# Differential heads between plain heads, `pv` taken out a step later, and the norm of the differential half inside the attention

## The reference, cut to what matters

```python
# plain heads (one block of 256 keys, so plain causal attention), q and k normed and rotated
p = softmax(mask(q @ k.T * 64 ** -0.5));  a = p @ v                       # 8 heads, v of width 64
a_out = rms_norm(a, moba_out_gain)                                        # over each head's 64
# differential heads: two maps of scores each
p0, p1 = softmax(mask(q0 @ k0.T / 8)), softmax(mask(q1 @ k1.T / 8))
b = (p0 - lam * p1) @ v                                                   # 4 heads, v of width 128
b_out = rms_norm(b, diff_out_gain) * (1.0 - lambda_init)                  # over each head's 128
x = x + concatenate([a_out, b_out]) @ w_out
x = x + peer_ffn(rms_norm(x, ffn_norm), ...)                              # experts
# second block, memory attention: keys and values of the memory, which need nothing of x
k, v = split(rmsnorm(mem, norm_mem_g) @ w_kv)
```

## Time and profile before

| | us |
|---|---|
| runs | 1474.99 median of 3, 1472.27 to 1475.25 |
| profiled execution, its own time | 1471.86 |
| its span in the trace | 1470.1 |
| busy in the span: PE, DVE, ACT, POOL | 1254.2, 801.9, 597.7, 904.9 |
| first scores, start of `xv0`, first `mixT` transpose, start of `w_out` | 99.37, 165.55, 182.82, 186.15 |
| TensorE idle before 162.43, released by DVE L1393 | 2.23 |
| ACT square of `att` (L984), 128 x 2048, at 166.47 | 1.92 |
| first gather, last product of the experts | 240.67, 930 |

### The profile page before, as it was taken

How to read it: one execution, slowest core, us unless ns; L and a number is a source line. 1 busy time by engine, 2 the same in 40 slices (tenths; PEclk the granted TensorE clock), 3 DMA queues, 4 the chain that set the end, 5 groups by cost and what they waited for, 6 DMA issues and landing times.

```text
span 1470.1 us, 17338 instructions
## 1 busy us (share of the span) xinstructions
PE 1254.2 (85%) x5876; PEld 891.1 (61%) x5876; DVE 801.9 (55%) x1514; ACT 597.7 (41%) x1249; POOL 904.9 (62%) x541
## 2 busy tenths in 40 slices
PE   7798697787976887787777787999999989999997
PEld 6577587533432333333333333689999968799886
DVE  5654427467677766677777744342254452268401
ACT  5455353423431333333323322345655435555432
POOL 6972568563536544444443452396878765599985
PEclk9998798899988998888989899999999999999999
DMA  7442257799999999999999999265554744455663
GB/s 266 130 150 86 82 184 259 301 412 419 373 421 420 420 421 420 421 420 421 420 421 420 418 420 399 84 191 167 172 158 133 227 141 131 130 173 187 199 187 100
DMA packets 72942, 400.68 MB, mean 273 GB/s; under 512 B 8096, under 2 KB 8352, under 8 KB 39712
## 3 DMA queue, kind: packets, MB, share of 16 engines
q0 software_dynamic: 36864, 268.45, 44.2%
q1 hardware_dynamic: 33696, 123.35, 26.5%
q10 hardware_dynamic: 2304, 7.85, 1.5%
HBM read 396.48 MB, written 3.15 MB: 272 GB/s over the span
## 4 chain that ended last, share of the span: by engine, by line
PE 29%; issue 18%; POOL 18%; DVE 17%; DMA 15%; ACT 2%; POOLq 0%; ACTq 0%; DVEq 0%
POOL w_lo L1175 15%; DMA arena<-in_experts,arena 11%; PE bank L713 9%; PE bank L526 6%; PE bank L527 6%; PE bank L528 6%; DVE arena L1492 4%; DMA late_rows<-in_experts,arena 4%; DVE arena L1440 1%; DVE arena L1444 1%; DVE arena L1442 1%; POOL arena L1222 1%; DVE arena L1443 1%; POOL stat L1149 1%; DVE arena L1439 1%
## 5 line engine op out<-in xcount | busy, mean ns | idle before, releaser
L1175 POOL TENSOR_TENSOR w_lo<-ring,w_hi 128x1024 fp32r<-128x1024 f32 x226 | 577.2, 2578 | 171.9 <-ACT w_hi L863 171.5
L713 PE MATMUL bank<-arena,diag 128*128 128x512 f32 x896 | 438.6, 648 | 117.0 <-ACT diag L1027 116.8
L1222 POOL DMA_INDIRECT arena<-in_experts,arena x224 | 255.7, 1142 | 288.4 <-PE bank L713 234.7
L713 PEld LDWEIGHTS bank<-arena,diag 128*128 128x128 f32 x896 | 183.2, 208 | 368.2 <-issue 231.0
L1492 DVE CUSTOM_DVE_ANT_0 arena<-arena 128x1024 f32<-128x1024 f32 x224 | 277.7, 1264 | 162.3 <-DMA arena<-in_experts,arena 158.5
L863 ACT ACTIVATE w_hi<-ring 128x1024 fp32r<-128x1024 f32 x228 | 240.6, 1059 | 215.3 <-PE bank L528 164.0
L526 PE MATMUL bank<-hT_hi,w_hi 128*128 128x256 f32 x736 | 210.4, 286 | 5.0 <-DVE hT_lo L1257 2.7
L527 PE MATMUL bank<-hT_lo,w_hi 128*128 128x256 f32 x736 | 209.1, 284 | 0.0
L528 PE MATMUL bank<-hT_hi,w_lo 128*128 128x256 f32 x736 | 209.0, 284 | 0.0
L1018 ACT ACTIVATE arena<-arena 128x4 f32<-128x4 f32 (+1 forms) x66 | 13.6, 205 | 441.2 <-DVE arena L1492 441.1
L526 PEld LDWEIGHTS bank<-hT_hi,w_hi 128*128 128x128 f32 x736 | 142.1, 193 | 6.3 <-issue 5.1
(11 more groups left out here) (231 smaller groups left out, 1772.9 us busy)
## 6 DMA issues: line engine op xcount, KB each, us to landing
ring<-in_stream SPq DMA_DIRECT2D x228, 512.0 KB, 3.5
arena<-in_experts,arena POOLq DMA_INDIRECT x224, 17.3
kv_park<-arena ACTq DMA_DIRECT2D x8, 256.0 KB, 4.5
arena<-kv_park ACTq DMA_DIRECT2D x1, 2048.0 KB, 8.8
x_res<-in_x SPq DMA_DIRECT2D x2, 512.0 KB, 5.2
arena<-in_mem SPq DMA_DIRECT2D x1, 1024.0 KB, 11.4
arena<-in_sub_keys ACTq DMA_DIRECT2D x1, 1024.0 KB, 6.2
out<-arena SPq DMA_DIRECT2D x2, 512.0 KB, 2.6
```

What stands on the lines that cost most here:

```text
L713: mm = pe.matmul(y_banks[half][:, :], diag[:, slot % DIAGS, :], rows_buf[BUFFER[slot]][:, D + 512 * half:D + 512 * half + 512], start=(i = ...
L1175: nc.gpsimd.tensor_tensor(w_lo[:, slot, :], ring[:, slot, :], w_hi[:, slot, :].bitcast(F32), ALU.subtract).then_inc(S("lo_made"), 1)
L1222: nc.gpsimd.indirect_dma_start(out=rows_buf[b], out_offset=None, in_=experts, in_offset=bass.IndirectOffsetOnAxis(ap=expert_u[:, slot:slot ...
```

## The change

It alters the order of the units, and three places that depend on it. The units are taken in the order 8, 0, 9, 1, 10, 2, 11, 3, 4, 5, 6, 7, so that the four differential heads stand between the first plain ones; the waits for `exps` and `maxes` count by the place of a map in this order. The fourth `xk` goes from step 12 to step 11. DVE takes `pv` of the unit of step s - 3 instead of s - 2, so its loop has 15 steps instead of 14. The norm of the differential half of `att` is done by itself: its squares in ACT's step 11, its sums in DVE's step 13, its inverse root on POOL first, its product in DVE's step 14. TensorE transposes `mixT` 2 and 3, which hold that half, ahead of `xv0`, and `mixT` 0 and 1 behind it; ACT and DVE split them in the same order. The operations and their sizes stay, but for the square, which is now two of half the size.

```diff
-MEMORY_STEPS = {("xk", 0): 2, ("xk", 1): 5, ("xk", 2): 8, ("xk", 3): 12, ("xv", 0): 16}
+HEAD_ORDER = [8, 0, 9, 1, 10, 2, 11, 3, 4, 5, 6, 7]
+MAP_ORDER = [m for unit in HEAD_ORDER for m in maps_of(unit)]
+MIX_ORDER = [2, 3, 0, 1]
+MEMORY_STEPS = {("xk", 0): 2, ("xk", 1): 5, ("xk", 2): 8, ("xk", 3): 11, ("xv", 0): 16}
...
 # TensorE; plan() follows the same order
             for step in range(16):
                 memory(step)
                 if step < 12:
-                    for m in maps_of(step):
+                    for m in maps_of(HEAD_ORDER[step]):
                         score(m)
                 if 3 <= step < 15:
-                    turn_probs(step - 3)
+                    turn_probs(HEAD_ORDER[step - 3])
                 if step >= 4:
-                    u = step - 4
+                    u = HEAD_ORDER[step - 4]
...
-            memory(16)
-            pe.wait_ge(S("att_normed"), 1)
-            for g in range(4):
-                turn(("mixT", g), ...)
+            for half in range(2):
+                pe.wait_ge(S("att_normed"), half + 1)
+                for g in MIX_ORDER[2 * half:2 * half + 2]:
+                    turn(("mixT", g), ...)
+                if half == 0:
+                    memory(16)
...
 # ACT
+            def att_square(units, cols):
+                for u in units:
+                    wait_evacuated(act, ("pv", u))
+                nc.scalar.activation(xn[:, :, cols], att[:, :, cols], ACT.Square).then_inc(S("att_squares"), 1)
...
                 memory_out(step + 2)
                 if step >= 1:
-                    u = step - 1
+                    u = HEAD_ORDER[step - 1]
                     copy_out(("pT", u), pT[:, u, :], n=SC)
+                if step == 11:
+                    att_square(range(8, 12), slice(512, 1024))
             memory_out(15)
             hi_parts(LAST["xv0"])
-            for u in range(4, 12):
-                wait_evacuated(act, ("pv", u))
-            nc.scalar.activation(xn, att, ACT.Square).then_inc(S("att_squares"), 1)
+            act.wait_ge(S("head_gain"), 1)
+            att_square(range(8), slice(0, 512))
+            for g in MIX_ORDER[:2]:
+                mix_hi(g)
             memory_out(16)
-            act.wait_ge(S("head_gain"), 1)
-            for g in range(4):
-                split_hi(("mixT", g), ...)
+            for g in MIX_ORDER[2:]:
+                mix_hi(g)
...
 # POOL
             lo_parts(LAST["xv0"])
+            pool.wait_ge(S("att_sums"), 1)
+            rsqrt(o_rs[:, 16:24], o_ss[:, 16:24], 1.0 / 128, S("att_rstd"))
             pool.wait_ge(S("att_sums"), 2)
             rsqrt(o_rs[:, 0:16], o_ss[:, 0:16], 1.0 / 64, S("att_rstd"))
-            rsqrt(o_rs[:, 16:24], o_ss[:, 16:24], 1.0 / 128, S("att_rstd"))
             norm("ffn")
...
 # DVE
-            for step in range(12 + 2):
+            for step in range(12 + 3):
...
+                if step == 13:
+                    dve.wait_ge(S("att_squares"), 1)
+                    v.tensor_reduce(o_ss[:, 16:24]..., xn[:, :, 512:1024]..., AX, ALU.add).then_inc(S("att_sums"), 1)
+                if step == 14:
+                    dve.wait_ge(S("att_rstd"), 1)
+                    v.tensor_tensor(a1, a1, r1..., ALU.mult).then_inc(S("att_normed"), 1)
-                if step >= 2:
-                    u = step - 2
+                if step >= 3:
+                    u = HEAD_ORDER[step - 3]
                     bank = take(dve, ("pv", u))
...
-            dve.wait_ge(S("att_squares"), 1)
+            dve.wait_ge(S("att_squares"), 2)
             v.tensor_reduce(o_ss[:, 0:16]..., xn[:, :, 0:512]..., AX, ALU.add).then_inc(S("att_sums"), 1)
-            v.tensor_reduce(o_ss[:, 16:24]..., xn[:, :, 512:1024]..., AX, ALU.add).then_inc(S("att_sums"), 1)
+            for g in MIX_ORDER[:2]:
+                mix_lo(g)
             dve.wait_ge(S("att_rstd"), 2)
-            own.link(v.tensor_tensor(a0, a0, r0..., ALU.mult))
-            v.tensor_tensor(a1, a1, r1..., ALU.mult).then_inc(S("att_normed"), 1)
-            for g in range(4):
-                split_lo(("mixT", g), ...)
+            v.tensor_tensor(a0, a0, r0..., ALU.mult).then_inc(S("att_normed"), 1)
+            for g in MIX_ORDER[2:]:
+                mix_lo(g)
```

More of the change, by code:

```diff
@@ L258, in split_order @@
         else:
-            keys += [(name, g) for g in range(2 if name in ("reT", "sbT") else 4)]
+            keys += [(name, g) for g in (MIX_ORDER if name == "mixT" else range(2 if name in ("reT", "sbT") else 4))]
     return {key: i + 1 for i, key in enumerate(keys)}
@@ L1368, in _, with mix_lo @@
             mask = o_c2["mask"]
[L1369 removed]
+            a0 = att[:, :, 0:512].rearrange("p t (h n) -> p t h n", n=64)
+            a1 = att[:, :, 512:1024].rearrange("p t (h n) -> p t h n", n=128)
+            r0 = o_rs[:, 0:16].rearrange("p (t h) -> p t h", t=TT)
+            r1 = o_rs[:, 16:24].rearrange("p (t h) -> p t h", t=TT)
+            def mix_lo(g):
+                ks = (2 * g, 2 * g + 1)
+                split_lo(("mixT", g), [hT_1[k] for k in ks], [ghead[:, k:k + 1] for k in ks])
+            for step in range(12 + 3):
                 if step < 12:
[L1371 removed]
+                    for m in maps_of(HEAD_ORDER[step]):
                         bank = take(dve, ("score", m))
```

43 lines of the change are left out of this document (20 added, 23 removed).

## The result

The changed kernel takes 1463.89 us (median of 4 runs, 1461.33 to 1466.83). The kernel before, run beside it, took 1473.63 (4 runs). The ratio is 0.9937, with a 95% interval of 0.9922 to 0.9952: 9.3 us faster, between 7.1 and 11.5. The forecast was 1465.2.

A forecast was written before the change was run, and what follows sets the result against it. It took the attention to be paced by TensorE, then by late differences, with the gathers bounding 287 to 930 us. w_out 11.2 us earlier, less 0.85 clock and 0.5 joints, gives 9.8: 1474.99 to 1465.2, range 1461 to 1468, with A 1471.5.

The forecast's parts named there:

- A later start: Start of attention: first scores wait for the seventh qkT copy, at 101.0 instead of 99.37, costing 1.6 us.
- The order of heads: Attention steps: plain work covers the differences, one 1.1 us late; last pT copy at 150.2, 13.7 us earlier, the large term.
- Results taken out a step later: VectorE's pv take-out: no price of its own, within the 13.7; without it about 0.3 us per plain step behind a stall.
- The norm's differential half: Before mixT 2: high part, low part, inverse root and 1.3 us product come onto the path; start at t0 + 7.0, 157.2.
- t0: End of ACT's last pT copy in the attention, forecast at 150.2, before at 163.9.
- rival C: Tail: t0 comes no earlier, while t0 to w_out loses 2.5 us, 4.2 with slow restart: 1479.2 us; chance 0.08.
- `xv0`, the copy-outs, `w_out`: Tail: xv0 ends 170.8, its 5.91 us idle go, copy-outs leave some 3 us idle, w_out at 175.0, 11.2 us earlier.
- The clock after that wait: Start of w_out after 3 us idle: half speed may cost 1.7 us; half of it, 0.85, taken.
- joints: Engine-to-engine delays that the walk leaves out: 0.5 us taken off the gain, between 0 and 3.
- w_out starts slow each time: Start of w_out: if the array is throttled by default, the sum is 0.85 us less.
- A: Rival, attention steps: the clock falls in gaps of about a microsecond, costing 4.5 us: 1469.7 us; chance 0.20.
- B, ACT sets the pace: Rival, attention: ACT's in-order queue costs eight steps a microsecond each, 8 us gone: 1473, no change; chance 0.12.

The follow-up runs named there:

- e2_pv_early: The changed kernel with VectorE taking the product with the values two steps late, as before, instead of three: 1478.5 us.
- e4_order_only: The kernel before with only the new order of heads and the fourth xk at step 11; product two steps late, old norm: 1474.6 us.
- e3_late_pv_only: The kernel before with one edit, the product with the values taken three steps late instead of two: 1458.9 us.
- e6_qkT_first: The changed kernel with the qkT transposes and copies reordered so that the two groups of map 8 come first: 1463.5 us.
- e5_root_first: The changed kernel with POOL's inverse root of the differential half moved ahead of the last low part of xv0: 1464.1 us.
- e1_norm_back: The changed kernel with the old norm: one square, sums and products behind the last pv, xv0 ahead of all mixT: 1459.1 us.
- e10_best_lag4: e9_best with the product with the values taken four steps late instead of three: 1451.0 us, 0.9847 of before.
- e9_best: Against the kernel before: product three steps late, plain half's norm begun inside the attention, mixT 0 and 1 split before xv0's copy-outs: 1455.0 us.

## Why the prediction came out right, and where its reasoning was wrong

The time was right (1465.2 for 1463.9) and so were nearly all places. The cause given for the largest term was wrong.

**A later start.** Forecast first scores at 101.0, measured 101.3 (104.11 less 2.85). The delay was right. That it could also cost clock was not in the sum: TensorE had to wait 1.80 us, the clock was at 0.50 from 106 to 108, and the first memory piece took 7.4 us for 5.9. It is not so each time: after 1.97 us idle in `e2_pv_early` and 1.81 in `e4_order_only` the clock stayed full.

**The order of heads.** Forecast end of the last `pT` copy 150.2, measured 150.5. Only one difference late, forecast 1.1 us, measured 0.70. The walk holds as a whole, partly because errors cancel. TensorE was done with step 4 at 114.0 (forecast 112.9), with step 6 at 123.9 (122.7), step 8 at 134.4 (133.7) and step 11 at 146.1 (145.5). The slow memory piece and the 0.3 us of a later start are 1.8 us; 0.7 of them are gone by step 4, 0.5 in step 7, where the difference was less late, and 0.3 more by the last copy.

**Results taken out a step later: the step that failed.** The prediction said: "this edit has no price of its own: it is in the 13.7. Without it the walk would be about 0.3 us longer in each plain step behind a stall". Without it the change takes 14.6 us more (`e2_pv_early`), and alone it gives 14.0 (`e3_late_pv_only`), with the last `pT` copy at 52.7 against the change's 52.4. The 13.7 us belong to this edit and none to the order. I walked only the kernel with both edits, and put its whole gain down to the one that I thought of as the large one. A walk of the old order with the late take-out could have told the two apart. The profile held the sign: TensorE's 4.46 us were read, but not VectorE's 5.50 us idle for TensorE just ahead of them, which says that the two hold each other up. Nor was it read that the gaps of a microsecond ahead of 134 are waits for VectorE's scores (L1373), the same tie in the plain heads.

**The norm's differential half.** Forecast `mixT` 2 at t0 + 7.0, measured 6.7 (153.34 to 160.04), with the fast product (1.3 forecast, 1.22 measured) since POOL was idle beside it. The Trainium skill ("GPSIMD Engine Reference", Specifications) was weighed there: GpSimd and VectorE share SBUF interfaces and contend where a VectorE instruction has two SBUF inputs. The trace agrees. The difference L1423 took 5.01 us with POOL's pieces beside it from 109.39, 2.72 the fourth time, and 0.75 the other two times, as at 118.98. The first was 4.3 us longer, more than the 2 us set aside for it. It delayed nobody here, but by 0.07 us only, and only because the memory piece ahead of it was slow (`e6_qkT_first`). `e5_root_first` shows the contention where it counts. The plain half's product, which the prediction expected slow by the same rule, took 1.23 us at 165.92: POOL's next piece started at 166.86, near its end.

**What the norm part is worth.** The prediction counted it as t0 to `w_out` 24.8 us for 22.3, so 2.5 lost. Measured 24.45 (153.34 to 177.79), and 3.1 us more than `e1_norm_back` needs for the same stretch. At `w_out` 2.0 of them show. From there to the first gather the change needs 56.0 us and `e1_norm_back` 55.1. With the slow restart it is 3.0 by the places and 4.8 by the medians, whose intervals of 2 to 3 us to either side allow both. So it is a loss inside a change that gains. The prediction had its 2.5 us, but only under rival C, and never asked what the change would be worth without this part.

**`xv0`, the copy-outs, `w_out`.** Forecast 170.8 for the end of `xv0`, ACT's two copy-outs late next, 3 us idle, `w_out` at 175.0. Measured 171.0, the copy-outs at 173.83 and 174.83, 3.12 us, and 174.9. The plain half was ready in time.

**The clock after that wait.** Half of 1.7 us was taken. TensorE restarted at 0.50, and up to about 180.9 the products took 0.63 in place of 0.39 to 0.40: 3.1 us at half speed, about 1.5 us lost. From `w_out` to the first gather the change needs 56.0 us, the kernel before 54.5: 1.5 us more, where the sum had 0.85 and 0.5 for joints. (The prediction's own stretch of 3.7 us at half speed is 1.85 us of work, not 1.7.) This is the case of "w_out starts slow each time": it did so in `e2_pv_early` too (0.77 for the first product after 3.13 us idle) and started at 0.47 after 0.69 us idle in `e10_best_lag4`. The rule of the Trainium skill ("TensorE: Matmul & The Clock Gate", What's actually happening), throttled by default and released by activity, fits these rows.

**The range.** Its upper end doesn't follow from its own terms: the slow product (nearly 2 us) and 3 us of joints for 0.5 give 1469.6, not 1468, and with A 1474, not 1471.5. The result doesn't turn on it.

**The rivals.** A, the clock within the steps: it fell once, at the first memory piece, for 1.5 us of the 4.5. B, ACT sets the pace: no. TensorE's waits for ACT from the first scores to the last `pv` are 1.80, 0.49 and 0.44 us. C, slower: its case, that the interleaving brings t0 forward by nothing, is what `e4_order_only` and `e2_pv_early` show. C gave 1479.2, and `e2_pv_early` took 1478.5. It did not decide because of the edit that was priced at nothing.

## What to carry to other kernels

When two in-order engines show idle time for each other in turn, look for the instruction on each that waits for a result it does not need yet, and move it back by a step or two. Here one such move was worth 14 us, and a reordering of all heads nothing that the times show. A walk of the changed schedule gives the total, not the causes: walk it once for each edit alone before saying which one pays. And when a step is moved to an engine's idle time, count what the partner engine does at that moment: the product that was moved beside a low part came out 2.7 times as long (3.35 for 1.22 us).

## What the runs showed of the hardware that was not expected

- TensorE's clock can fall after less than 2 us of idleness, but need not. After 1.80 us idle in front of the first scores it was at 0.50 from 106 to 108 (and in `e1_norm_back` after 1.81 us at 0.50 from 102 to 108). After 1.97 us in `e2_pv_early` and 1.81 in `e4_order_only` it stayed at 1.00. After 1.38 us before 137.01 it fell to 0.50 in `e3_late_pv_only`, and after 1.39 us before 111.93 in `e6_qkT_first` it stayed at 1.00. So the length of a gap alone does not say what it costs.
- VectorE and GpSimd hold each other up, and which of them waits goes with which started first. The product of 128x1024 took 1.22 us alone. It took 3.35 us (`e5_root_first`) where POOL's low part had started 0.07 us ahead of it, 2.74 where the part had started 0.74 us ahead (`e9_best`, 158.39) and 1.85 where it had started 1.62 us ahead (`e10_best_lag4`, below). Each of the three ended 1.1 us after POOL's piece. The pair of L1423 took 5.01 us for 0.75 beside two pieces that had started 0.07 us earlier, and 2.86 in `e1_norm_back`, where the second piece began 0.65 us after the first had ended. The other way round POOL waits: its operation at 154.03 takes 1.06 us for 0.20 and ends with VectorE's product. In the kernel before, three low parts beside the two slow products take 8.94 us, where one alone takes 2.4. `e10_best_lag4`, both engines, then POOL in the kernel before:

```profile
151.56 2.38 POOL L1191 TENSOR_TENSOR w_lo<-ring,w_hi 128x1024 fp32r<-128x1024 f32 x1
153.18 1.85 DVE L1446 TENSOR_TENSOR arena<-arena,stat 128x1024 f32<-128x1024 f32 x1
154.03 1.06 POOL L1163 TENSOR_SCALAR stat<-stat 128x8 f32<-128x8 f32 x1
```

```profile
176.04 8.94 POOL L1175 TENSOR_TENSOR w_lo<-ring,w_hi 128x1024 fp32r<-128x1024 f32 x3
```
